# Cached attention of one decode step: block transposes of the latents on VectorE, scores as 32-row tiles, eight pages a step

## What is computed

```python
past_c = cache_kv_latent[page_table]          # (8, 4096, 256)
past_r = cache_k_rope[page_table]             # (8, 4096, 32)
q_lat = einsum('bqhd,chd->bqhc', q_nope, w_a_uk)
sc_past = (einsum('bqhc,bkc->bhqk', q_lat, past_c)
           + einsum('bqhd,bkd->bhqk', q_rope, past_r)) * ATTN_SCALE
p = softmax(concatenate([sc_past, sc_new], axis=-1), axis=-1)
o_lat = einsum('bhqk,bkc->bqhc', p_past, past_c) + einsum('bhqk,bkc->bqhc', p_new, c_kv)
o = einsum('bqhc,chd->bqhd', o_lat, w_a_uv)
```

## Time and profile before

| | |
|---|---|
| median of 3 runs | 1607.82 us (1606.84 to 1608.46) |
| the profiled execution, span | 1607.8 us |
| TensorE busy | 1583.7 us, 98% |
| TensorE weight loads | 1406.4 us, 87% |
| VectorE busy | 939.4 us, 58% |
| ScalarE busy | 587.1 us, 37% |
| GpSimd busy | 192.1 us, 12% |
| DMA moved | 109.18 MB, mean 68 GB/s |

### The profile page before, as it was taken

One profiled execution on the slowest core, in us unless ns is written; L12 is line 12 of the kernel. 1 busy time (PEld: TensorE's weight loads), 2 busy tenths in 40 slices (PEclk: granted clock), 3 DMA queues, 4 the chain that ended last, 5 costly groups with the idle time before them and its releaser, 6 DMA issues. The chain is left out here.

```text
span 1607.8 us, 29621 instructions
## 1 busy us (share of the span) xinstructions
PE 1583.7 (98%) x10341; PEld 1406.4 (87%) x10341; DVE 939.4 (58%) x1818; ACT 587.1 (37%) x1281; POOL 192.1 (12%) x297
## 2 busy tenths in 40 slices
PE   8999999999999999999999999999999999999998
PEld 7988888888886556667889999999999999999996
DVE  5666666666664555546666455544546455455547
ACT  5465565555653333323233131121312213131136
POOL 2000000000001410000003112020211202122000
PEclk9999999999999999999999999999999999999999
DMA  6111111011115765523122020120202111020103
GB/s 227 42 31 30 28 24 25 13 28 26 31 46 168 234 193 163 172 90 95 53 78 80 27 66 21 57 65 26 65 13 65 61 30 53 26 65 14 39 27 119
DMA packets 150583, 109.18 MB, mean 68 GB/s; under 512 B 54623, under 2 KB 139293, under 8 KB 150352
## 3 DMA queue, kind: packets, MB, share of 16 engines
q1 hardware_dynamic: 148272, 100.95, 21.6%
q0 software_dynamic: 1776, 5.71, 1.2%
q10 hardware_dynamic: 432, 1.21, 0.2%
HBM read 101.88 MB, written 10.14 MB: 70 GB/s over the span
## 5 line engine op out<-in xcount | busy, mean ns | idle before, releaser
L1979 PE MATMUL banks<-act_hi,up_hi 128*128 128x352 f32 (+2 forms) x1040 | 335.5, 323 | 0.7 <-PEq L1551 0.7
L1980 PE MATMUL banks<-act_lo,up_hi 128*128 128x352 f32 (+2 forms) x1040 | 335.1, 322 | 0.0
L1981 PE MATMUL banks<-act_hi,up_lo 128*128 128x352 f32 (+2 forms) x1040 | 334.9, 322 | 0.0
L1979 PEld LDWEIGHTS banks<-act_hi,up_hi 128*128 128x128 f32 x1040 | 195.5, 188 | 1.0 <-issue 0.9
L1980 PEld LDWEIGHTS banks<-act_lo,up_hi 128*128 128x128 f32 x1040 | 195.3, 188 | 0.0
L1981 PEld LDWEIGHTS banks<-act_hi,up_lo 128*128 128x128 f32 x1040 | 195.2, 188 | 0.0
L2282 DVE TENSOR_TENSOR o_t<-o_t,banks 128x352 f32<-128x352 f32 x240 | 120.9, 520 | 94.5 <-PE banks L1981 94.2
L2261 DVE SCALAR_TENSOR_TENSOR conv_out<-conv_in,conv_now,conv_out 128x1072 f32<-128x1072 f32 x42 | 63.7, 1517 | 185.6 <-ACT conv_out L2135 185.6
L1056 DVE TENSOR_REDUCE neg_max<-banks 128x1 f32<-128x896 f32 (+7 forms) x128 | 96.6, 755 | 111.3 <-PE banks L828 110.4
L2126 ACT ACTIVATE conv_in<-banks 128x352 f32<-128x352 f32 x84 | 36.3, 458 | 336.2 <-PE banks L1981 336.2
L1979 PE MATMUL banks<-gated_hi,down_hi 128*128 128x352 f32 x480 | 155.8, 325 | 0.0
(11 more groups left out here) (339 smaller groups left out, 3111.2 us busy)
## 6 DMA issues: line engine op xcount, KB each, us to landing
weight_stage<-in_w_f_up SPq DMA_DIRECT2D x44, 512.0 KB, 4.7
c_stage<-in_cache_kv_latent SPq DMA_DIRECT2D x140, 128.0 KB, 2.3
down_stage<-in_w_f_down SPq DMA_DIRECT2D x22, 512.0 KB, 4.2
head_weights_stage<-in_cache_kv_latent SPq DMA_DIRECT2D x56, 128.0 KB, 2.2
rope_query_tab<-in_cache_kv_latent SPq DMA_DIRECT2D x56, 128.0 KB, 2.3
rope_rows<-in_cache_k_rope SPq DMA_DIRECT2D x256, 16.0 KB, 2.0
wo_stage<-in_w_a_out POOLq DMA_DIRECT2D x8, 512.0 KB, 4.5
z<-in_x_prompt SPq DMA_DIRECT2D x8, 512.0 KB, 3.6
```

Of the source, the lines that this page charges most:

```text
L1979: nc.tensor.matmul(o, ws[0], xs[0], start=first, stop=False)
L1980: nc.tensor.matmul(o, ws[0], xs[1], start=False, stop=False)
L1981: return nc.tensor.matmul(o, ws[1], xs[0], start=False, stop=last)
```

## The change

In `attend`: VectorE writes each finished output block to a small staging buffer, and GpSimd stores it to memory (`o_blocks`), 32 stores. The rope gather moves 256-byte runs, 37 pages for each pair of heads where there were 32. Five fills are loaded before `decode` instead of two. In the last pair of heads VectorE transposes the keys of the first item, and GpSimd builds the query blocks of the first pair.

In `decode`: an item is two fills, so that there are 16 items of 1024 positions per sequence, and the new tokens join the first item of each pair. There are eight slots. A page goes into 64 partitions, 2 KB each. SyncE issues five pages of each fill, GpSimd three. VectorE transposes raw pages in blocks of 32 x 32 straight from the slot into `xt`, five instructions for an item. The scores take 32 rows a product: nine row blocks (eight of latents, one of rope) x two sequences x four row groups = 72 products of 256 columns, each for 64 output partitions and one of four banks. GpSimd lays out the queries for them (24 copies per pair). ScalarE, not VectorE, copies the transposed probabilities. Three of the eight row blocks of the output weight are split late, by ScalarE and VectorE.

In `mix`: the prompt tiles are loaded from memory before they are split. Semaphores are reused between stages. `ffn` does the same work as before. The diff, cut to its core:

```diff
-SLOTS = 5
+STEPS = NG // 2
+SLOTS = 8
+LATE_WO = (5, 6, 7)
+KEY_ROWS = (KV_LORA + ROPE) // 32
+GATHERS = 37
+BY_SP = [(0, 0), (0, 1), (0, 2), (0, 3), (1, 0)]
+BY_POOL = [(1, 1), (1, 2), (1, 3)]
+FIRST_KEYS_AT = {10: (0, 0), 11: (0, 1), 12: (1, 0), 13: (1, 1), 14: "rope"}
+def page_load(io, m, eng, f, some, landed):
+    for b, j in some:
+        at = f * 8 + b * 4 + j
+        page = eng.value_load(m.pages[0:1, at:at + 1])
+        rows_, c = slice(64 * (j % 2), 64 * (j % 2) + 64), (b * 2 + j // 2) * 2 * KV_LORA
+        eng.dma_start(m.slot[f % SLOTS][rows_, c:c + 2 * KV_LORA], io["cache_kv_latent"][bass.ds(page, 1)]
+                      .rearrange("o (p k) c -> p (o k c)", k=2)).then_inc(landed, 16)
+def keys_t(nc, dve, m, n, part):
+    x = m.xt[n % 2].rearrange("p (j c) -> p j c", j=KEY_ROWS)
+    if part == "rope":
+        dve.wait_ge(m.r_in[n % 2], 16 * (n // 2 + 1))
+        nc.vector.transpose(x[:, KEY_ROWS - 1, :], m.r_slot[n % 2][:, :]).then_inc(m.x_ok, 1)
+        return
...
+    raw = m.slot[f % SLOTS][:, b * 4 * KV_LORA:(b + 1) * 4 * KV_LORA].rearrange("p (v j a) -> p v j a", v=4, a=32)
+    out = x[:, 0:KEY_ROWS - 1, half * 256 + b * 128:half * 256 + (b + 1) * 128].rearrange("p j (v k) -> p v j k", v=4)
+    nc.vector.transpose(out, raw).then_inc(m.x_ok, 1)
+def queries(nc, m, q):
+    for i in range(4):
+        for g in range(4):
+            nc.gpsimd.tensor_copy(qj[rows_, g:KEY_ROWS - 1:4, :], ...)
+        for b in range(2):
+            last = nc.gpsimd.tensor_copy(qj[rows_, KEY_ROWS - 1, 64 * b:64 * b + 64], ...)
@@ attend, GpSimd
+            def store_o(p, g):
+                pool.wait_ge(of_ok, n + 1)
+                pool.dma_start(m.o_blocks[2 * g:2 * g + 2, :, p, :]..., staged_o[:, n % 2, :]...)
@@ decode, SyncE
+            for i in range(2):
+                sp.wait_ge(m.o_st[i], 16 * 2 * PAIRS)
+            for f in range(5, FILLS):
                 if f >= SLOTS:
-                    sp.wait_ge(pv, fill_item(f - SLOTS) + 1)
+                    sp.wait_ge(pv, f - SLOTS + 1)
+                sp_pages(io, m, sp, f)
+                if f % 2 == 0 and f >= 6:
+                    rope_load(io, m, sp, f // 2 - 1)
@@ decode, GpSimd
+            queries(nc, m, 1)
+            for f in range(5, FILLS):
+                if f >= SLOTS:
+                    pool.wait_ge(pv, f - SLOTS + 1)
+                pool_pages(io, m, pool, f)
+                if f >= 9 and f % 4 == 1 and k < LATE_WO[0]:
+                    pool.dma_start(wst[:, :], io["w_a_out"][k * P:(k + 1) * P, :]).then_inc(wo_in, 16)
+                if f >= 9 and f % 4 == 2 and k < LATE_WO[0]:
+                    nc.gpsimd.tensor_copy(m.wo_hi[:, k, :], wst[:, :]).then_inc(wo_hi, 1)
+                    nc.gpsimd.tensor_tensor(m.wo_lo[:, k, :], wst[:, :], f32(m.wo_hi[:, k, :]), ALU.subtract)
+                if f in (15, 23):
+                    queries(nc, m, (f + 1) // 8)
@@ decode, TensorE
+                for j in range(KEY_ROWS):
+                    for b in range(2):
+                        for i in range(4):
+                            r = slice(32 * i, 32 * i + 32)
+                            last = nc.tensor.matmul(ps[64 * b:64 * b + 64, i, half(n)], qj[r, j, b, :], x[r, j, :, b, :],
+                                                    start=j == 0, stop=j == KEY_ROWS - 1)
+            new_scores()
             scores(0)
-            tiles(1)
             for n in range(ITEMS):
-                if n + 2 < ITEMS:
-                    tiles(n + 2)
+                if n:
+                    values(n - 1)
                 transposes(n)
                 if n + 1 < ITEMS:
                     scores(n + 1)
@@ decode, VectorE
             for n in range(ITEMS):
+                row_max(n)
+                keys_ahead(n + 2, KEY_PARTS[0:2])
+                if n:
+                    update(n - 1)
+                denominators(n)
+                keys_ahead(n + 2, KEY_PARTS[2:5])
```

More of the change, by code:

```diff
@@ L162, in project @@
         x_in = [s("x_in0"), s("x_in1")]
-        w_in = [s(f"wd_in{i}") for i in range(WS)]
+        w_in = m.w_in
         c_in, g_in, out_l = s("p_consts"), s("p_gains"), m.out_l
@@ L1132, in _ @@
                         w.split_lo(nc, dve, p + 1, SPLIT_AT[n])
+                    if not more and n in FIRST_KEYS_AT:
+                        keys_t(nc, dve, m, 0, FIRST_KEYS_AT[n])
                 if more:
@@ L1267, in _, with new_scores @@
         @block.tensor
         def _(pe):
+            def new_scores():
+                for q in range(DPAIRS):
+                    out = ps[:, NB, q * N_SAMPLE:(q + 1) * N_SAMPLE]
+                    for k in range(KC):
+                        nc.tensor.matmul(out, m.qlt[:, k, 2 * q:2 * q + 2, :].rearrange("p b c -> p (b c)"),
+                                         m.cknew[:, k, :], start=k == 0, stop=False)
+                    last = nc.tensor.matmul(out, sr[0:2 * ROPE, q, :, :].rearrange("p b c -> p (b c)"), m.rtnew[:, :],
+                                            start=False, stop=True)
+                last.then_inc(new_ps, 1)
@@ L1319, in transposes @@
             def transposes(n):
-                q, step = item(n)
+                q, first = n // STEPS, n % STEPS == 0
                 pe.wait_ge(ex, n + 1)
@@ L1397, in _ @@
             last.then_inc(uv, 1)
-            out_first(7, 2 * KD)
+            out_first(8, 2 * KD)
         @block.scalar
@@ new lines, in exp, with probs_t @@
+                src = ps[:, 0:4, half(n)].rearrange("p i (v k) -> p i v k", v=8)
+                nc.scalar.activation(prob[:, :].rearrange("p (v i k) -> p i v k", v=8, i=4), src, ACT.Exp, bias=neg[:, i:i + 1],
+                                     accum_out=rs[:, i:i + 1]).then_inc(ex, 1)
+                if not first:
+                    nc.scalar.activation(al[:, i:i + 1], neg[:, 1 - i:2 - i], ACT.Exp, bias=neg[:, i:i + 1], scale=-1.0).then_inc(al_ok, 1)
+            def probs_t(n):
+                act.wait_ge(pt_ps, n + 1)
+                if n:
+                    act.wait_ge(pv, 2 * n)
+                if n % STEPS == 0:
+                    copy(pt_new[:, :], ps[0:N_SAMPLE, NB, 0:P])
+                for h in range(2):
+                    last = copy(pt[:, 4 * h:4 * h + 4, :], ps[:, PB + h, :].rearrange("p (v c) -> p v c", v=4))
+                last.then_inc(pt_ok, 1)
@@ L1586, in _ @@
             load_x(1)
+            for t in range(4, TT - 1):
+                load_o(m, sp, t)
             for k, name in enumerate(("ln_g", "ln_b")):
```

616 lines of the change are left out of this document (327 added, 289 removed).

## The result

The changed kernel takes **1580.05 us** (median of 4 runs, 1579.63 to 1583.12) against 1608.13 (1606.84 to 1608.46) for the kernel before, run beside it: ratio 0.983, 95% interval 0.982 to 0.984. The direction was forecast right, but 1537 was predicted and even the range of 1524 to 1575 missed it. The profiled execution spans 1581.4 us. Its new stage, from the old edge at 487.3 us to the first product of the mix stage at 701.07, takes 213.8 us. Before it took 244.3; forecast were 171.

A forecast was written before the change was run, and what follows sets the result against it. TensorE was taken to bound the kernel. Start 18.5, fourteen items 124.6, tail 23.6 and late pages 4 give a 171 us stage against 244.3: 73 saved, 2 given back, so 1537 us; range 1524 to 1575.

The forecast's parts named there:

- TensorE's part: TensorE's work per decode item: scores 4.1 us, values 3.6, probability transposes 0.95, together 8.65 against 13.34 before.
- both rivals about the records: Decode scores: records no faster than 54 ns, about 1590 us (0.08); or tiles only two at a time, 1700 us (0.04).
- the half-paced transposes: Rival: VectorE's block transposes in decode take 2.5 us each, VectorE needs 13.6 us an item, 1598 us total (0.05).
- The prediction's own sign: In decode, TensorE waiting for the exponential in every item would show that the chain within an item isn't covered.
- I put the item at 8.9: Decode item length by SyncE's poorer issuing pace, instead of TensorE's 8.65 us; fourteen items make 124.6 us.
- The 0.81 us a page: SyncE's issuing price per decode page; ten pages and the rope load take 8.6 us, at the poorer pace 8.9.
- SyncE begins ahead: In decode, 27 fills are left and five lie ready, so SyncE starts early, but free slots limit its lead.
- covered, by 0.6: Decode's maximum and exponential take 3.0 us with signals, while TensorE does 3.6 us of values.
- 309 GB/s: DMA rate for decode's 35 MB, 247 divided by share 0.80: 113 us of some 135 available.
- 18.5 forecast: Decode's start: wait of 1.32 us, new tokens' scores 4.6, item 0 5.1, then waits, transposes and item 1's scores.
- if that cover went, some 4 us: Mix stage's first tile loads: out_first and the samples' products give 12 us of cover; costed at nothing, otherwise 4 us.
- The rival of late data: Decode: SyncE, GpSimd, DMA or VectorE ends last; items of 10.3 us give 1558, up to 11 us 1568 (0.20).

The follow-up runs named there:

- e1: Changed kernel with each rope load issued before the pages of its own item's first fill, about 15 us earlier: 1571.6 us.
- e4: Changed kernel with half the page bytes from fill 8 on, as many loads: 1571.0 us.
- e5: Changed kernel with early rope loads (e1) and half the page bytes from fill 8 on (e4): 1567.3 us.
- e7: e1 with GpSimd taking up the weight block two fills later: 1571.8 us.
- e9: Changed kernel with VectorE's maximum of the next step ahead of the second half of the key transposes two steps ahead: 1575.4 us.
- e16: Changed kernel with each rope load issued ahead of one fill's wait and five pages, 5 to 8 us earlier: 1574.4 us.
- e14: Changed kernel with each page load waiting for half a step's values more than needed before taking a slot: 1602.5 us.
- e10: e6 with VectorE's maximum first as in e9: 1557.0 us.
- e6: e1 with each page laid over 128 partitions, 1 KB in each, instead of 64 with 2 KB: 1563.6 us.
- e2: Changed kernel with the attention's last store issued by SyncE instead of GpSimd: 1579.6 us.

## Why the prediction was wrong, point by point

- **TensorE's part was right.** Scores 4.14 us for 144 records (4.1), values 3.67 (3.6), transposes 1.04 to 1.09 (0.95). So both rivals about the records are out, and the half-paced transposes too: two block transposes take 2.37 us, the rope one 0.71, against 1.15 each and 0.6. VectorE has some 8 us of work a step, not 7.6. The prediction's own sign came: TensorE waits for the exponential in ten of the steps (28.1 us), so the chain isn't covered.
- **The term that failed is the item: "I put the item at 8.9".** It measured 11.73. Fourteen take 164.3 us, where the forecast had 124.6 and 4 for late pages, 35.7 us less. Two steps of the working are in it.
- **First, SyncE's price.** The 0.81 us a page, and so the 8.9 us, were read from the kernel before, whose pages go to 128 partitions. With pages of 64 partitions by 2 KB the instruction takes 0.469 us instead of 0.333, ten pages, the rope load and the gaps 10.3 us (544.13 to 554.39). At 1.4 us a step this is some 20 of the 35.7 us. Nearly every experiment ran into it: e1, e4, e5, e7, e9 and e16 have steps of 10.8 to 11.4 us with 10.4 to 10.7 of SyncE's own. No run changes this price alone.
- **Second, the overlap.** The forecast compared what each engine and queue has to do in a step (8.65, 7.6, 8.9, 5.4 us) and took the largest. That holds only if each can work ahead. "SyncE begins ahead" and the chain within an item, "covered, by 0.6", were each looked at alone. The chain that runs through all of them and closes, from a freed slot over five pages, a rope load, its landing, a maximum, an exponential, transposes and scores to the values that free the next, was never added up. The eight slots suggested four steps of lead. VectorE transposes two steps ahead and the values come a step behind the scores, so hardly one was left. It shows as SyncE's waits for slots, 22.7 us. Less the 4 us that were allowed, and with the 20 above, this is about 38 us, near enough to the 35.7. e14 shows that the loop closes, e1 and e16 its tightest place, and e10 steps of 8.7 us where both parts are out of the way.
- **The DMA rate was carried over from another layout.** 309 GB/s came from dividing 247 by its share of 0.80, for pages of 128 partitions by 1 KB. For that layout e6 and e10 bear the division out (272 GB/s at 0.88, 286 at 0.90). The pages in the new layout run at 231 to 253 at a share of about 1, and the argument that 2 KB runs lie nearer to the first 20 us had the wrong sign. Full queues also cost landing time: a page took 4.1 us instead of 2.3.
- **GpSimd.** Its page was right at 0.9. Its lateness was named (3 to 6 us, three times) but is 6 to 8 where it shows, and the share of four and four would have been worse. That its transfers wait behind VectorE's block transposes doesn't show in the landing: its pages land after 4.2 us (middle value), SyncE's after 4.1.
- **Edges.** Start: 18.5 forecast, 25.9 measured, of which 4.4 are the barrier behind GpSimd's store, taken as 0.54, and 3 are the new tokens' and item 0's scores at the lower clock (a mean of 0.50 and 0.62). Tail: 23.6 forecast, 23.6 measured. The attention gave back nothing instead of 2.
- **The mix stage** was costed at nothing, "if that cover went, some 4 us". It grew by 3.5 us in this profile, and by 1.3 to 4.7 in the others with this order. It wasn't the cover for the first tiles that went: VectorE waits for the gain loads, since SyncE issues four loads ahead of them.
- **The sum:** the stage's terms come to 170.7 us, and 213.8 is 43.1 more, in the steps (35.7) and the start (7.4). With 3.5 from mix and 0.6 behind it, less the 2 of the attention, this is the 45.2 us between the profiled 1581.4 and the 1536.2 that the unrounded terms give. The rival of late data had the right family, and SyncE first in its list; it named rope nowhere and allowed items up to 11 us and 1568.
- **The clock.** The prediction had full clock for all items. Behind four of TensorE's waits (at 529.6, 552.7, 587.9 and 660.7 us) part of the scores ran on the lower level: they took 5.5 to 6.2 us instead of 4.14, together 6.5 us, on top of the late load that made TensorE wait. The granted clock over these scores was 0.65 to 0.78. Behind two more waits (at 574.9 and 634.8 us) the scores lost another 0.6 and 2.0 us, at 0.86 and 0.81. No run isolates this.

## What to carry to other kernels

Price the issuing of a transfer in the layout that it will have: a change of layout moved 10 loads a step from 0.333 to 0.469 us each on the queue that issues them, and that queue became the bound. A queue's time doesn't stand in the table of busy engines, so count it beside them: what it issues in a step, with the gaps, and how much of the step it waits for anything.

When a stage runs on a ring of buffers, don't stop at the busiest engine either. Follow one buffer from its release through the issue, what is queued ahead on the issuing engine, the landing, and every in-order engine up to the use that releases the next, and divide by the steps in that turn. Then look at what stands behind a wait in each engine's program: a wait for data two steps ahead must not stand before work whose inputs are ready.

## What the runs showed of the hardware

- A barrier came 4.2 us after the last store that GpSimd had issued, and 4.1 us after it in e2, where that was the store before. TensorE's wait was 3.16 instead of 6.24 us.
- A 128 KB page load took SyncE's queue 0.469 us as 64 partitions of 2 KB, and 0.333 us as 128 partitions of 1 KB, before the change and again in e6 (middle values of 100 to 140). Halving the bytes (e5) left SyncE's time for a step at 10.59 us.
- 128 KB pages as 64 partitions of 2 KB ran at 231 to 253 GB/s with a DMA share of 0.93 to 1.04, and as 128 partitions of 1 KB at 272 to 282 with 0.88.
- Eight 32-row tiles at once hold 144 records in 4.14 us, 29 ns each with their weight loads, half of the 54 ns that was the densest row before.
- A VectorE operation on 128 x 256 that takes 0.35 us (at 599.51) took 2.35 us at 553.93 and ended with GpSimd's subtraction, which ran from 553.78 to 556.13: a second case of what the earlier trace rows shows.
- Gaps named "issue" can hide a wait for a semaphore that another engine raised (4.79 us in e9). Shorter ones inside a group of scores, where nothing is waited for (1.60 us at 642.97 in the changed kernel, 2.95 us at 538.38 in e9), came while the DMA queues were busy. What holds TensorE there is open.
